# The values of Fox attention: probabilities stationary in one piece, or values stationary in two column halves with the result turned back

## What is computed

```python
f = log_sigmoid(f_logit); c = cumsum(f, axis=tokens)
s = (q @ k.T) * 64 ** -0.5 + c[query] - c[key]      # masked where key > query
o = softmax(s) @ v                                  # per head, 512 x 64
```

## Time and profile before

| what | us |
|---|---|
| median of three runs | 1470.57 |
| the profiled execution | 1469.13 |
| its span in the profile | 1467.3 |
| start of the first Fox scores in the span | 257.35 |
| start of the last Fox values' last record | 303.1 |
| start of the output projection's first product | 309.68 |

### The profile page before, as it was taken

How to read it: one execution, slowest core, us unless ns; L and a number is a source line. 1 busy time by engine, 2 the same in 40 slices (tenths; PEclk the granted TensorE clock), 3 DMA queues, 4 the chain that set the end, 5 groups by cost and what they waited for, 6 DMA issues and landing times.

```text
span 1467.3 us, 19785 instructions
## 1 busy us (share of the span) xinstructions
PE 1408.8 (96%) x7358; PEld 1112.2 (76%) x7361; DVE 593.4 (40%) x1130; ACT 610.0 (42%) x1151; POOL 626.2 (43%) x345
## 2 busy tenths in 40 slices
PE   6999999999999999999999998898999999999999
PEld 5787887778778786666786687785788888888887
DVE  1104103632362245777343777979322332332000
ACT  4222222634123237888353565455344443433210
POOL 2763533563446523332335662520134344434441
PEclk9999999999999999999999999999999999999999
DMA  6553532012225420112223231102022323232330
GB/s 196 118 100 96 115 104 68 2 38 86 74 85 162 125 72 1 38 37 81 58 73 131 72 108 48 69 8 109 29 87 86 100 86 100 87 99 90 97 115 29
DMA packets 78399, 120.25 MB, mean 82 GB/s; under 512 B 8448, under 2 KB 41392, under 8 KB 77936
## 3 DMA queue, kind: packets, MB, share of 16 engines
q1 hardware_dynamic: 76096, 114.21, 26.8%
q0 software_dynamic: 2208, 4.98, 1.2%
q10 hardware_dynamic: 16, 0.00, 0.0%
HBM read 114.95 MB, written 4.19 MB: 81 GB/s over the span
## 4 chain that ended last, share of the span: by engine, by line
PE 77%; issue 8%; POOL 5%; DVE 3%; ACT 3%; DMA 2%; DVEq 1%; POOLq 1%; SPq 0%; ACTq 0%
PE psum L1695 20%; PE psum L1697 20%; PE psum L1696 20%; POOL weight_low L490 4%; PE psum L1707 3%; PE psum L1727 3%; PE psum L1758 3%; PE psum L1674 1%; PE psum L1869 1%; PE psum L2070 1%; PE psum L2046 1%; PE psum L1856 1%; POOL rstd L514 1%; PE psum L1741 1%; DVEq L1422 1%
## 5 line engine op out<-in xcount | busy, mean ns | idle before, releaser
L490 POOL TENSOR_TENSOR weight_low<-weight_raw,weight_high 128x1024 fp32r<-128x1024 f32 x188 | 459.1, 2446 | 614.5 <-ACT weight_high L710 312.5
L1695 PE MATMUL psum<-act_ring,weight_high 128*128 128x512 f32 x704 | 281.9, 400 | 0.3 <-issue 0.3
L1697 PE MATMUL psum<-act_ring,weight_low 128*128 128x512 f32 x704 | 278.5, 396 | 0.0
L1696 PE MATMUL psum<-act_ring,weight_high 128*128 128x512 f32 x704 | 277.8, 395 | 0.0
L710 ACT ACTIVATE weight_high<-weight_raw 128x1024 fp32r<-128x1024 f32 x104 | 110.0, 1060 | 387.7 <-PE psum L1697 378.7
L1695 PE MATMUL psum<-weight_high,act_ring 128*128 128x512 f32 x480 | 193.5, 403 | 2.8 <-DVE odd_k L1302 2.3
L1697 PE MATMUL psum<-weight_high,act_ring 128*128 128x512 f32 x480 | 190.2, 396 | 0.0
L1696 PE MATMUL psum<-weight_low,act_ring 128*128 128x512 f32 x480 | 190.1, 396 | 0.0
L1695 PEld LDWEIGHTS psum<-act_ring,weight_high 128*128 128x128 f32 x704 | 132.8, 189 | 36.4 <-issue 5.4
L1697 PEld LDWEIGHTS psum<-act_ring,weight_low 128*128 128x128 f32 x704 | 132.6, 188 | 33.1
L1696 PEld LDWEIGHTS psum<-act_ring,weight_high 128*128 128x128 f32 x704 | 132.8, 189 | 31.3
(11 more groups left out here) (352 smaller groups left out, 2128.9 us busy)
## 6 DMA issues: line engine op xcount, KB each, us to landing
weight_raw<-in_w_ffn_in SPq DMA_DIRECT2D x88, 256.0 KB
weight_raw<-in_even_w_in SPq DMA_DIRECT2D x32, 512.0 KB
weight_raw<-in_w_in SPq DMA_DIRECT2D x24, 512.0 KB
weight_raw<-in_w_ffn_out SPq DMA_DIRECT2D x22, 512.0 KB
weight_raw<-in_odd_w_in SPq DMA_DIRECT2D x20, 512.0 KB
weight_raw<-in_even_w_out SPq DMA_DIRECT2D x8, 512.0 KB
weight_raw<-in_odd_w_in SPq DMA_DIRECT2D x16, 256.0 KB
weight_raw<-in_odd_w_out SPq DMA_DIRECT2D x8, 512.0 KB
```

The lines of the kernel that those rows point to most:

```text
L490: nc.gpsimd.tensor_tensor(WL[:, r], RAW[:, r], WH[:, r].bitcast(f32), ALU.subtract).then_inc(split_ready, 1)
L1695: mm(bank, hi_l, hi_r, start=start, stop=False, skip_group_check=True)
L1696: mm(bank, hi_l, lo_r, start=False, stop=False, skip_group_check=True)
L1697: return mm(bank, lo_l, hi_r, start=False, stop=stop, skip_group_check=True)
```

## The change

Fox attention takes the way of the odd layer. `pair_values` goes; `half_values` is numbered from the first step of all and is called at the even steps from 4, `pair_back` at steps 7, 11, 15 and 19, and TensorE's loop has one step more. ScalarE has `pair_copy` at steps 6, 10, 14 and 18 (its loop has one step more). VectorE's division waits for `pair_back` and reads the result in the other order. The transposed probabilities of two steps stay until the half is used: of the first two steps of a pair in `A_PT`, of the other two in columns 512 to 1023 of `even_v`, which held the retention's values. The copied result (`fox_pair_t`) lies where the small weights' high and low parts are at other times. The waits of the copies (`half_free`) are for the values of four steps before.

```diff
--- before.py
+++ after.py
@@ -131,6 +131,10 @@
+        lay_m = ExitStack()
+        sb(lay_m, "small_raw_stays", [P, NK, SMALL])
+        F_OT = sb(lay_m, "fox_pair_t", [P, 2, T])
+        lay_m.close()
@@ -350,6 +354,8 @@ def probs_t(s, h)
             if s // 2 % 2 == 0:
                 half = A_PT[:, h].rearrange("p a (b q) -> p (a b) q", b=2)
+            elif s < FOX_UNITS:
+                half = E_V[:, :, 512 + 2 * P * h:768 + 2 * P * h]
             elif s < SEC_FIRST:
@@ -359,15 +365,14 @@ def pair_t(p)
+            if p < FOX_UNITS // 4:
+                return F_OT[:, p % 2, :]
             return O_OT[p % 2][:, :] if p < SEC_FIRST // 4 else S_OT[:, p % 2, :]
 
         def half_free(eng, s):
 
-            n = (s - FOX_UNITS) // 2
-            if n >= 2:
-                eng.wait_ge(sem("half_values"), n - 1)
-            elif n >= 0:
-                eng.wait_ge(sem("pair_values"), FOX_UNITS)
+            if s >= 4:
+                eng.wait_ge(sem("half_values"), s // 2 - 1)
@@ -756,8 +761,8 @@ def pair_copy(s, first)
-                if first and s >= first + 6 and last == 0:
-                    act.wait_ge(sem("half_values"), 2 * (p - FOX_UNITS // 4) + 2)
+                if s >= first + 6 and last == 0:
+                    act.wait_ge(sem("half_values"), 2 * p + 2)
                     nc.scalar.activation(pair_t(p), PS[:, 6 + p % 2, :], ACT.Copy).then_inc(sem("pair_out"), 1)
@@ -766,15 +771,9 @@ def pair_exp(s, first, last)
-                    if k >= FOX_UNITS:
-                        half_free(act, k)
-                        nc.scalar.activation(probs_t(k, 1)[1], ...)
-                    else:
-                        if k >= 2:
-                            act.wait_ge(sem("pair_values"), k - 1)
-                        nc.scalar.activation(A_PT[:, k % 2, 1, 0:n], PS[:, 5, 0:n], ACT.Copy).then_inc(
-                            sem("pair_pt_b"), 1)
+                    half_free(act, k)
+                    nc.scalar.activation(probs_t(k, 1)[1], ...)
@@ -891,7 +890,7 @@
-            for s in range(FOX_UNITS + 2):
+            for s in range(FOX_UNITS + 3):
                 pair_exp(s, 0, FOX_UNITS)
@@ -1147,26 +1146,17 @@ def pair_step(s0, steps, s, take_pair)
-                    if k >= FOX_UNITS:
-                        half_free(dve, k)
-                        v.tensor_copy(probs_t(k, 0)[1], ...)
-                    else:
-                        if k >= 2:
-                            dve.wait_ge(sem("pair_values"), k - 1)
-                        v.tensor_copy(A_PT[:, k % 2, 0, 0:n], PS[:, 4, 0:n]).then_inc(sem("pair_pt"), 1)
+                    half_free(dve, k)
+                    v.tensor_copy(probs_t(k, 0)[1], ...)
...
                 if s >= s0 + 7 and last == 0:
-                    if s0:
-                        dve.wait_ge(sem("pair_back"), p - FOX_UNITS // 4 + 1)
-                    else:
-                        dve.wait_ge(sem("pair_values"), 4 * p + 4)
+                    dve.wait_ge(sem("pair_back"), p + 1)
                     v.reciprocal(RSUM[:, :], PSUM[:, p % 4, :])
@@ -1728,25 +1718,11 @@
-            def pair_values(k, value):
-
-                p, q = k // 4, step_tile(k)
-                if k % 4 == 0 and p:
-                    pe.wait_ge(sem("pair_done"), p - 1)
-                for h in range(2):
-                    pe.wait_ge(sem("pair_pt_b" if h else "pair_pt"), k + 1)
-                    at = 4 * HD * h + HD * q
-                    nt = step_width(k) // P
-                    for t in range(nt):
-                        last = mm(PS[:, 6 + p % 2, at:at + HD], A_PT[:, k % 2, h, P * t:P * t + P], value(h, t),
-                                  start=t == 0, stop=t == nt - 1, skip_group_check=True)
-                last.then_inc(sem("pair_values"), 1)
-
             def half_values(n, value):
 
-                s0 = FOX_UNITS + 2 * n
+                s0 = 2 * n
                 p, late = s0 // 4, n % 2
-                if not late:
+                if p >= 2 and not late:
                     pe.wait_ge(sem("pair_done"), p - 1)
@@ -1872,7 +1848,7 @@
-            for s in range(FOX_UNITS + 3):
+            for s in range(FOX_UNITS + 4):
@@ -1883,11 +1859,13 @@
                 if 2 <= s < FOX_UNITS + 2:
                     pair_turn(s - 2)
-                if s >= 3:
-                    p = (s - 3) // 4
-                    if s - 3 in (0, 4):
+                if s >= 4 and s % 2 == 0:
+                    p = s // 4 - 1
+                    if s in (4, 8):
                         pe.wait_ge(sem("ret_taken"), 3 + p)
-                    pair_values(s - 3, lambda h, t, p=p: E_V[:, t, P * p + HD * h:P * p + HD * h + HD])
+                    half_values(s // 2 - 2, lambda h, t, p=p: E_V[:, t, P * p + HD * h:P * p + HD * h + HD])
+                if s >= 7 and s % 4 == 3:
+                    pair_back((s - 7) // 4)
             features("even_y")
```

More of the change, by code:

```diff
@@ L768, in pair_exp @@
                     n = step_width(k)
[L769 to L777 removed]
+                    half_free(act, k)
+                    nc.scalar.activation(probs_t(k, 1)[1], PS[:, 5, 0:n].rearrange("p (t q) -> p t q", q=P),
+                                         ACT.Copy).then_inc(sem("pair_pt_b"), 1)
                 if s >= last:
@@ L1149, in pair_step @@
                     dve.wait_ge(sem("pair_turned"), 2 * k + 1)
-                    if k >= FOX_UNITS:
-                        half_free(dve, k)
-                        v.tensor_copy(probs_t(k, 0)[1], PS[:, 4, 0:n].rearrange("p (t q) -> p t q", q=P)).then_inc(
-                            sem("pair_pt"), 1)
-                    else:
-                        if k >= 2:
-                            dve.wait_ge(sem("pair_values"), k - 1)
-                        v.tensor_copy(A_PT[:, k % 2, 0, 0:n], PS[:, 4, 0:n]).then_inc(sem("pair_pt"), 1)
+                    half_free(dve, k)
+                    v.tensor_copy(probs_t(k, 0)[1], PS[:, 4, 0:n].rearrange("p (t q) -> p t q", q=P)).then_inc(
+                        sem("pair_pt"), 1)
                 if s < s0 + steps:
@@ L1161, in pair_step @@
                 if s >= s0 + 7 and last == 0:
-                    if s0:
-                        dve.wait_ge(sem("pair_back"), p - FOX_UNITS // 4 + 1)
-                    else:
-                        dve.wait_ge(sem("pair_values"), 4 * p + 4)
+                    dve.wait_ge(sem("pair_back"), p + 1)
                     v.reciprocal(RSUM[:, :], PSUM[:, p % 4, :])
                     v.drain()
-                    order = "p (t h d) -> p h t d" if s0 else "p (h t d) -> p h t d"
-                    take_pair(p, PS[:, 6 + p % 2, :].rearrange(order, h=2, t=4))
+                    take_pair(p, PS[:, 6 + p % 2, :].rearrange("p (t h d) -> p h t d", h=2, t=4))
             def per_head(cols):
@@ L1763, in pair_back @@
             def pair_back(p):
-                pe.wait_ge(sem("pair_out"), p - FOX_UNITS // 4 + 1)
+                pe.wait_ge(sem("pair_out"), p + 1)
                 for t in range(NT):
@@ L2023, in _ @@
                     col = 256 * SNAKE[i % 2][gp][0] + HD * i
-                    half_values(u // 2 - 2, lambda h, t, col=col: O_V[:, t, col:col + HD])
+                    half_values(s // 2 - 2, lambda h, t, col=col: O_V[:, t, col:col + HD])
                 if u >= 7 and u % 4 == 3:
@@ L2184, in _ @@
                         pe.wait_ge(sem("hg_squared"), 4)
-                    half_values((s - 4 - FOX_UNITS) // 2, lambda h, t, k=s - 4: sec_value(k, h, t))
+                    half_values(s // 2 - 2, lambda h, t, k=s - 4: sec_value(k, h, t))
                 if s >= SEC_FIRST + 7 and s % 4 == 3:
```

2 lines of the change are left out of this document (removed).

## The result

| what | before | after |
|---|---|---|
| median of 16 runs each, us | 1469.87 | 1466.24 |
| ratio, 95% interval | | 0.9974 [0.9967, 0.9980] |
| the profiled execution / its span, us | 1469.13 / 1467.3 | 1466.22 / 1464.4 |
| first Fox scores to the first product, us | 52.33 | 50.05 |
| first product to the end of the span, us | 1157.6 | 1156.6 |

The kernel became faster by 2.9 to 4.9 us, as forecast, and 1466.24 lies inside the range. In the trace the Fox stage gave 2.3 us of it and not the 3.15 that the sum had. The two traces can be laid over each other at four points: the first scores, step 6's scores, step 15's scores, and the first product of the output projection.

A forecast was written before the change was run, and what follows sets the result against it. TensorE was taken to bound the Fox stage, GpSimd its end. Cheaper values less shape changes gave 4.3 us, less 1.1 of waits 3.2; 1470.57 less 3.15 made 1467.4 us, range 1465.6 to 1469.6.

The forecast's parts named there:

- the sum: Whole kernel: the Fox stage's gain, 3.15 us, taken as passed on whole to the total.
- The halves: TensorE's Fox values: early half 0.80, late half 1.66, way back 0.59 us, replacing 4.62 us of values a pair.
- Rival 4: Fox stage: the two column halves don't overlap, a pair takes 1.2 us more, total 1475.4 us; chance 0.03.
- Changes of tile shape: TensorE between transposes and other products: 0.08 us for each of four turns, 0.32 us a pair.
- The gain without waits: Fox stage up to step 15: 4.3 us gained if TensorE never waits.
- Waits for the exponentials: TensorE's scores wait for ScalarE: 0.55 us at step 4, 0.2 at step 6, 0.2 at step 10.
- Waits for VectorE's copy: TensorE waits for VectorE's copy of probabilities behind the group norm's sums: 0.15 us, at steps 13 and 14.
- rival 2: Fox pairs: VectorE and ScalarE, the copying engines, become the bound; gain 1.95 us, time 1468.6 us; chance 0.20.
- The end: Fox stage's end: pair 3's serial chain ends at 301.9, GpSimd's last gate still comes later, by 0.6 us.
- The clock: Fox stage: forecast counted no added low stretch; granted clock was 0.96 over the stage, 1.00 in its pairs.
- rival 3: Fox stage: the clock falls after step 4's wait, costing at most 1.9 us, time 1469.3 us; chance 0.07.
- The total: Whole kernel: 1467.4 us against the median 1470.57, just over the 0.2% edge.

The follow-up runs named there:

- after_order: Kernel after with each Fox half multiplied head after head instead of the two heads in turn; 1470.19 us, ratio to before 0.9998.
- after_order2: The same kernel as after_order, run once more for its trace; one run, 1469.24 us.
- after_high: Kernel after with ScalarE's key and query parts of pairs 2 and 3 moved one step later; 1465.67 us, ratio to before 0.9971.
- after_nostat: Kernel after without VectorE's two small scalings on 8 columns after the group norm's sums; 1463.76 us, ratio to before 0.9955.
- after_gate: Kernel after with GpSimd's gate of pair 2 moved ahead of its wait for the fourth mean_gn; 1466.28 us, ratio to before 0.9969.
- before_again: Kernel before run again, unchanged; 1469.38 us, ratio to before 0.9995.
- after_split: Kernel after with the squares' sums moved from steps 4, 8, 12 and 16 to 6, 10, 14 and 16; 1466.79 us, ratio to before 0.9981.
- before_keep: Kernel before with eight products of zeros on TensorE in its wait for GpSimd at the Fox stage's end; 1469.08 us, ratio to before 0.9994.
- before_gate: Kernel before with GpSimd's gate of pair 2 moved ahead of its wait for the fourth mean_gn; 1468.61 us, ratio to before 0.9989.
- after_best: Kernel after with squares' sums at steps 6, 10, 12 and 16 and GpSimd's gate of pair 2 moved earlier; 1464.76 us, ratio to before 0.9967.

## Why the prediction was right, and which term was not

**The halves: right.** 0.80 and 1.66 in Fox, as in the odd layer; the way back 0.53 where 0.59 was counted. The 2.31 for both halves, which the prediction set beside its row, did not come. Rival 4's reason against itself (eight records in 0.80 us "with 256 columns") was loosely read, as the last key tile's records stream 128; that the halves overlap is shown by the starts of their records 7 ns apart. after_order and after_order2 show that the late half's 1.66 rests on the two heads being taken in turn.

**Changes of tile shape: right.** The sets of 8, 6, 4 and 2 transposes take 0.97, 0.76, 0.56 and 0.22 us. At 0.88 for eight they would take 0.88, 0.66, 0.44 and 0.22, so the changes cost 0.09 + 0.10 + 0.12 = 0.31 a pair, against 0.32 counted.

**The gain without waits: right.** 2.29 us were gained from step 3 (263.65, 264.10) to step 15 (295.45, 293.61). The waits named below add up to 2.05. Together 4.34, against 4.3.

**Waits for the exponentials: right.** Step 4 waited 0.86 - 0.31 = 0.55, as said. Step 6 waited 269.33 to 270.29, 0.96 where six transposes take 0.76: 0.2, as said. Step 10 0.3, against 0.2. after_high shows that those of steps 6 and 10 were ScalarE's key and query parts; step 4's stays there.

**Waits for VectorE's copy: the term that was mis-sized.** The prediction gave 0.15 us in all, at step 14 alone ("step 13 has the copy and step 14 the transposes that need the bank"). Measured were 0.20 at step 6, 0.54 at step 10 and 0.27 at step 14, 1.0 together. The earlier trace rows did show the copy behind the sums, at 281.11. What was left out is that the same burst comes at every fourth step, and how far it reaches once steps 8 and 9 are 1 us shorter (281.76 - 276.43 = 5.33 before, 280.06 - 275.74 = 4.32 after): the copy's time is set by VectorE's own queue and GpSimd's operations, and does not shorten with TensorE's. after_nostat took two of its operations away and got 1.07 back between step 6 and step 15. The sum of waits is 2.05 instead of 1.1, the gain at step 15 2.3 instead of 3.2. For the same reason GpSimd's fourth inverse root came 1.84 us earlier (298.40) and not 3.2, and the first product at 307.85 and not 306.5, 0.45 of it by a later start of the stage. This is half of rival 2 (VectorE, in bursts); its other half, ScalarE's copy as a bound, did not come: the copy shown above is done 0.53 us ahead of the way back, where the prediction had 0.2, and the way back is late only for the last pair.

**The end: right.** GpSimd's fourth inverse root starts 298.40 - 293.61 = 4.79 after step 15's scores, as 4.8 before. The last gate needs a division that ends at 303.2 and starts at 303.84 (298.40, 300.18, 301.36, 302.59 and 1.25 for one gate): a cover of 0.6, where after_gate measured about 0.5. The late half without cover, two waits of 0.67 and 0.69 us for ScalarE, cost nothing, as they lie under GpSimd.

**The clock: right for after.** Its granted clock is 1.00 from 264 us to the first product. But what rival 3 described exists at another place, the end of the stage, in some executions of either kernel (before_again, after_split), at 0.6 to 1.1 us.

**The total: near by luck in part.** 1466.24 is 1.16 below 1467.4. Of that 0.70 is the median of before, 1469.87 over 16 runs and not 1470.57 over three; the rest is a gain of 3.63 instead of 3.15. By the stage it should have been 2.3. A faster later stage does not explain the 1.3 us between (before_again), and before_keep could not show a loss of before at the end of the stage. The part behind the first product alone varies between 1154.8 and 1157.6 us among the traces of before, before_again, before_gate and before_keep.

The executions themselves show a part of the answer, by the clock granted over the whole of each. All executions of the two unchanged kernels for which it is recorded:

| mean granted clock | before: executions, mean us | after: executions, mean us | difference |
|---|---|---|---|
| 0.990 to 0.992 | 21, 1468.3 | 10, 1465.7 | 2.6 |
| 0.988 | 41, 1469.8 | 12, 1466.8 | 3.0 |
| 0.986 and 0.987 | 22, 1471.5 | none | |

At the same clock the two kernels lie 2.6 to 3.0 us apart, so 0.6 to 1.0 of the 1.3 us comes from executions of before at a lower clock, of which after had none. Whether the change makes them rarer is not shown: before_again, the same kernel as before, had none in eleven either, and after_gate had four of seven at 0.987. The other 0.3 to 0.7 stays open. So the total came out near the forecast in part by an amount that no step of it had.

## What to carry to other kernels

When work is taken from the engine that bounds, write down for each step which operation of the others it needs and where that stands in their queues: their bursts (here a group norm's sums every fourth step) keep their place, and the saved time turns into waits for whatever stands behind them. Count such a burst at every step where it returns, with the durations that its operations have beside a busy GpSimd. And before moving one of its parts, ask who waits for it at the end: the cut that saved TensorE 1.08 us gave it all back on GpSimd until the third sum kept its place. And compare two kernels at the same granted clock before a difference of 1 us is explained.

## What the runs showed of the hardware that was not expected

- An operation of VectorE on 128x8 took 0.17 us alone and 0.48 to 0.65 beside GpSimd in after, each time until GpSimd's operation ended.
- Of two column halves, records that alternate between the heads take 1.66 us for 16, head after head 2.57; for 8 records the two orders take 0.80 and 0.81. Head after head, the second head's first record starts beside the record four places ahead of it, and not earlier.
- The same program had a stretch of 1.2 GHz at 307 us in one execution and not in another (0.64 us), and one at the start of the stage that before_gate and after_best lacked (about 1.3 us from the first scores to step 6). Of the two traces of the kernel before, one has 2.7 us less behind the first product: a single trace tells a change of this size only stage by stage.
- Over a whole execution, the kernel before took 1468.3 us on average at a mean granted clock of 0.990 to 0.992, 1469.8 at 0.988 and 1471.5 at 0.986 and 0.987.
